# Attention units of a two-block transformer kernel: logits of tiles 0 and 1 in one group, later tiles a period sooner, stick-breaking values by two

## What is computed

```
layer a: gMLP spatial gating + memory attention (4 heads of 64, 256 memory rows) -> w_out -> conv FFN
layer b: forgetting attention (12 heads, causal, decay bias) + memory attention   -> w_out -> conv FFN
layer c: stick-breaking attention (8 heads) + differential attention (4 heads, two maps each,
         ALiBi bias, p1 - lam * p2, RMS norm of the output), both gated by silu   -> w_out
```

## Time and profile before

| | us |
|---|---|
| median of three executions | 1449.86 |
| lowest, highest | 1449.11, 1451.22 |
| the profiled execution | 1451.27 |
| its span from first to last instruction | 1449.5 |
| PE busy | 1438.8 (99%) |
| DVE busy | 961.8 (66%) |
| ACT busy | 669.5 (46%) |

### The profile page before, as it was taken

How to read it: one execution, slowest core, us unless ns; L and a number is a source line. 1 busy time by engine, 2 the same in 40 slices (tenths; PEclk the granted TensorE clock), 3 DMA queues, 4 the chain that set the end, 5 groups by cost and what they waited for, 6 DMA issues and landing times.

```text
span 1449.5 us, 20006 instructions
## 1 busy us (share of the span) xinstructions
PE 1438.8 (99%) x7041; PEld 1151.6 (79%) x7041; DVE 961.8 (66%) x1579; ACT 669.5 (46%) x1100; POOL 41.0 (3%) x82
## 2 busy tenths in 40 slices
PE   8999999999999999999999999999999999999999
PEld 7978888888888887777778888888888877777777
DVE  5656777777766647555556777777677666666774
ACT  7445444444442235445454444444323356665662
POOL 0000000000001110000000000000111000000000
PEclk9999999999999999999999999999999999999999
DMA  6323222332346733212132322323677511112122
GB/s 227 124 96 117 73 90 98 101 97 91 101 138 236 235 112 119 76 59 88 61 100 73 101 90 98 101 90 115 203 241 234 163 56 59 59 58 74 59 82 94
DMA packets 44445, 162.66 MB, mean 112 GB/s; under 512 B 5076, under 2 KB 5844, under 8 KB 44384
## 3 DMA queue, kind: packets, MB, share of 16 engines
q1 hardware_dynamic: 33984, 126.44, 26.5%
q0 software_dynamic: 9104, 33.06, 6.7%
q10 hardware_dynamic: 1296, 2.36, 0.4%
HBM read 159.72 MB, written 2.12 MB: 112 GB/s over the span
## 4 chain that ended last, share of the span: by engine, by line
PE 93%; DVE 4%; DMA 2%; ACT 1%; issue 1%; POOL 0%; ACTq 0%; DVEq 0%; POOLq 0%
PE ps L383 17%; PE ps L384 17%; PE ps L385 17%; PE ps L399 5%; PE ps L401 5%; PE ps L400 5%; PE ps L1872 3%; PE ps L1874 3%; PE ps L1873 3%; PE ps L486 3%; PE ps L563 2%; PE ps L2050 1%; PE ps L551 1%; PE ps L1806 1%; PE ps L1808 1%; DVE wl L309 1%
## 5 line engine op out<-in xcount | busy, mean ns | idle before, releaser
L309 DVE TENSOR_TENSOR wl<-raw,wh 128x1024 fp32r<-128x1024 f32 (+3 forms) x199 | 253.9, 1276 | 119.0 <-ACT wh L303 118.8
L303 ACT CAST wh<-raw 128x1024 fp32r<-128x1024 f32 (+3 forms) x199 | 217.7, 1094 | 228.1 <-PE ps L385 194.8
L383 PE MATMUL ps<-xh,wh 128*128 128x512 f32 x720 | 281.1, 390 | 0.6 <-DVE hb L1416 0.6
L385 PE MATMUL ps<-xh,wl 128*128 128x512 f32 x720 | 280.2, 389 | 0.0
L384 PE MATMUL ps<-xl,wh 128*128 128x512 f32 x720 | 280.1, 389 | 0.0
L383 PEld LDWEIGHTS ps<-xh,wh 128*128 128x128 f32 x720 | 135.1, 188 | 30.0 <-issue 2.0
L384 PEld LDWEIGHTS ps<-xl,wh 128*128 128x128 f32 x720 | 135.1, 188 | 28.3 <-issue 0.5
L385 PEld LDWEIGHTS ps<-xh,wl 128*128 128x128 f32 x720 | 135.1, 188 | 28.2
L399 PE MATMUL ps<-xh,wh 128*128 128x512 f32 x344 | 144.5, 420 | 0.7 <-DVE wl L309 0.7
L383 PE MATMUL ps<-hth,wh 128*128 128x512 f32 x352 | 136.9, 389 | 0.0
L384 PE MATMUL ps<-htl,wh 128*128 128x512 f32 x352 | 136.9, 389 | 0.0
(11 more groups left out here) (310 smaller groups left out, 2337.3 us busy)
## 6 DMA issues: line engine op xcount, KB each, us to landing
raw<-w_a_f SPq DMA_DIRECT2D x44, 512.0 KB, 3.2
raw<-w_b_f SPq DMA_DIRECT2D x44, 512.0 KB, 3.2
row<-w_c_rows POOLq DMA_DIRECT2D x32, 512.0 KB, 4.6
row<-w_ada_rows POOLq DMA_DIRECT2D x24, 512.0 KB, 4.7
raw<-w_a_f SPq DMA_DIRECT2D x16, 704.0 KB, 4.1
raw<-w_b_f SPq DMA_DIRECT2D x16, 704.0 KB, 4.2
raw<-w_b_pair SPq DMA_DIRECT2D x18, 512.0 KB, 3.3
raw<-w_front SPq DMA_DIRECT2D x16, 512.0 KB, 3.3
```

The costliest lines, as they stand in the source:

```text
L303: nc.scalar.copy(wh[:, s, :width], raw[:, s, :width]).then_inc(w_hi, 1)
L309: nc.vector.tensor_tensor(wl[:, s, :width], raw[:, s, :width], wh[:, s, :width].bitcast(F32), ALU.subtract).then_inc(w_lo, 1)
L383: nc.tensor.matmul(dst, a, h(k), start=(k == 0), stop=False)
L385: mm = nc.tensor.matmul(dst, b, h(k), start=False, stop=(k == total - 1))
```

## The change

- `PAIR_AT`, `AHEAD_AT` and `MEM_AT` say in which step the logits of which tile are written. In all units those of tiles 0 and 1 are written at t = 0. `fx` and `df` units write those of tiles 2 and 3 at t = 2 and 4 (before: 4 and 6), memory units both at t = 4 (before: 4 and 6), stick-breaking units at t = 4 and 6 as before. DVE's max (`low`) and ACT's exps (`soft`) follow in the same steps; `norm` (`softplus`), `turned` (`tri`) and `copy` stay where they are.
- `lg_at` puts the second tile of such a pair into the same bank, right of the first, if both fit (128+256 columns, or 256+256). `lg_last` makes the max of the first tile wait until the logits of the second are written too, and in memory units the exps of the first wait for the max of the second.
- The values of stick-breaking units are multiplied by two tiles, at the end of t = 5 and 9; a second buffer `awt` holds the weights of odd tiles.

```
+        PAIR_AT, AHEAD_AT, MEM_AT = {0: (0, 1), 4: (2,), 6: (3,)}, {0: (0, 1), 2: (2,), 4: (3,)}, {0: (0, 1), 4: (2, 3)}
+        def lg_at(i, nk):
+            n0 = nk(i - 1) if i % 2 and nk(i - 1) + nk(i) <= S else 0
+            return slice(n0, n0 + nk(i))
+        def lg_last(i, nk):
+            return i + 1 if i + 1 < TT and lg_at(i + 1, nk).start else i
...
         for t in range(PE_STEPS):
             i, odd = divmod(t, 2)
-            if not odd and i < TT:
-                logits(i)
+            for e in lg_in.get(t, ()):
+                logits(e)
...
-                if not odd:
-                    for s in (2 * i - 2, 2 * i - 1):
-                        if i >= 1:
-                            copy(s)
-                    for s in (2 * i, 2 * i + 1):
-                        if i < TT:
-                            exps(s)
+                if not odd and i >= 1:
+                    copy(2 * i - 2)
+                    copy(2 * i - 1)
+                for e in lg_in.get(t, ()):
+                    exps(2 * e)
+                    exps(2 * e + 1)
...
-                if i < TT:
-                    for s in (2 * i, 2 * i + 1):
-                        norm(s) if odd else maxs(s)
+                for e in lg_in.get(t, ()):
+                    maxs(2 * e)
+                    maxs(2 * e + 1)
+                if odd and i < TT:
+                    norm(2 * i)
+                    norm(2 * i + 1)
...
-                dve.wait_ge(a["logit"], 8 * it + s + 1)
+                dve.wait_ge(a["logit"], 8 * it + 2 * lg_last(s // 2, nk) + s % 2 + 1)
...
-                    if not odd and jj < TT:
-                        soft(2 * jj)
-                        soft(2 * jj + 1)
+                    for e in PAIR_AT.get(t, ()):
+                        soft(2 * e)
+                        soft(2 * e + 1)
...
-                pe_pairs(z, tri, pv, between_last(u), u == 0)
+                pe_pairs(z, tri, pv, between_last(u), u == 0, pv_at={2: (0, 1), 4: (2, 3)})
```

More of the change, by code:

```diff
@@ L481, in norm_factor, with pair_logits @@
             dve.wait_ge(s_r, k + 1)
-        def pair_logits(i, n, q, k, last):
+        PAIR_AT, AHEAD_AT, MEM_AT = {0: (0, 1), 4: (2,), 6: (3,)}, {0: (0, 1), 2: (2,), 4: (3,)}, {0: (0, 1), 4: (2, 3)}
[4 more added lines that the diff above has]
+            return i + 1 if i + 1 < TT and lg_at(i + 1, nk).start else i
+        def pair_logits(i, nk, q, k, last):
             for h in range(2):
-                mm = nc.tensor.matmul(lg[h][:, :n], q(h, i), k(h, n), start=True, stop=last)
+                mm = nc.tensor.matmul(lg[h][:, lg_at(i, nk)], q(h, i), k(h, nk(i)), start=True, stop=last)
             return mm
@@ L490, in turn_bank, with pe_pairs @@
             return lg[1] if a is att["fx"] and it == 5 and s == 7 else tb[s % 2]
-        def pe_pairs(logits, turned, values, between, behind_first=False, pv_at={1: (0,), 2: (1,), 3: (2,), 4: (3,)}):
+        def pe_pairs(logits, turned, values, between, behind_first=False, pv_at={1: (0,), 2: (1,), 3: (2,), 4: (3,)}, lg_in=PAIR_AT):
             for t in range(PE_STEPS):
                 i, odd = divmod(t, 2)
-                if not odd and i < TT:
-                    logits(i)
+                for e in lg_in.get(t, ()):
+                    logits(e)
                 if behind_first and t == 2:
@@ L521, in act_pairs, with dve_pairs @@
                 behind(t)
-        def dve_pairs(maxs, norm, behind, rest=None):
+        def dve_pairs(maxs, norm, behind, rest=None, lg_in=PAIR_AT):
             for t in range(PE_STEPS - 1):
                 i, odd = divmod(t, 2)
-                if i < TT:
-                    for s in (2 * i, 2 * i + 1):
-                        norm(s) if odd else maxs(s)
+                for e in lg_in.get(t, ()):
[4 more added lines that the diff above has]
+                    norm(2 * i + 1)
                 if t == 1 and rest:
@@ L536, in logits @@
             def logits(i):
-                n = nk(i)
-                wait(pe, a["max" if decayed else "exp"], 8 * it + 2 * i)
-                mm = pair_logits(i, n, q, k, not decayed)
+                own = lg_at(i, nk)
+                wait(pe, a["max" if decayed else "exp"], 8 * it + 2 * (i if own.start == 0 else i - 1))
+                mm = pair_logits(i, nk, q, k, not decayed)
                 if not decayed:
@@ L543, in logits @@
                 for h in range(2):
-                    nc.tensor.matmul(lg[h][:, n - P:n], identb, maskq, start=False, stop=True).then_inc(a["logit"], 1)
+                    nc.tensor.matmul(lg[h][:, own.stop - P:own.stop], identb, maskq, start=False, stop=True).then_inc(a["logit"], 1)
             def turned(s):
@@ L566, in values @@
                             mm.then_inc(a["pv"], 1)
-            pe_pairs(logits, turned, values, between, pv_at={2: (0, 1), 4: (2, 3)})
+            pe_pairs(logits, turned, values, between, pv_at={2: (0, 1), 4: (2, 3)}, lg_in=AHEAD_AT if decayed else MEM_AT)
         def two_act(act, a, it, p, pt, nk, behind, rest=None, decayed=False):
@@ L572, in exps @@
                 n = nk(s // 2)
-                act.wait_ge(a["max"], 8 * it + s + 1)
+                act.wait_ge(a["max"], 8 * it + (s if decayed else 2 * lg_last(s // 2, nk) + s % 2) + 1)
                 if decayed:
@@ L586, in copy @@
                 nc.scalar.copy(pt[s // 2 % 2][:, s % 2, :n], turn_bank(a, it, s)[:, :n]).then_inc(a["copy"], 1)
-            act_pairs(exps, copy, behind, rest)
+            act_pairs(exps, copy, behind, rest, AHEAD_AT if decayed else MEM_AT)
         def shifted_max(src, bias, dst, s):
@@ L613, in norm @@
                                         ALU.mult).then_inc(a["norm"], 1)
-            dve_pairs(maxs, norm, behind, rest)
+            dve_pairs(maxs, norm, behind, rest, AHEAD_AT if decayed else MEM_AT)
         def mix_high(act, m, k, src, s_ready, v_ready):
@@ L1153, in weight @@
                     act.wait_ge(Z["tri"], base + s + 1)
-                    wait(act, Z["pv"], base + s - 1)
-                    nc.scalar.activation(aws[:, s % 2, :w], zb[s % 4][:, :w], ACT.Exp).then_inc(Z["a"], 1)
+                    wait(act, Z["pv"], base + s - 3)
+                    nc.scalar.activation((aws, awt)[s // 2 % 2][:, s % 2, :w], zb[s % 4][:, :w], ACT.Exp).then_inc(Z["a"], 1)
                 def high(s):
@@ L2035, in z @@
                     j, w = 3 - jj, (jj + 1) * P
-                    wait(pe, Z["a"], base + 2 * jj - 2)
+                    wait(pe, Z["a"], base + (2 * jj - 2 if jj > 1 else 0))
                     for h in range(2):
@@ L2098, in values @@
                     mm.then_inc(a["pv"], 1)
-                pe_pairs(logits, turned, values, between_last(u))
+                pe_pairs(logits, turned, values, between_last(u), lg_in=AHEAD_AT)
             out_block("c_out", *OUT_EARLY[30])
```

24 lines of the change are left out of this document (12 added, 12 removed).

## The result

The changed kernel takes 1455.20 us (median of five, 1454.68 to 1457.29) where the kernel before, in executions beside it, takes 1449.98: a ratio of 1.0038, with a 95% interval of 1.0026 to 1.0050. By the ratio it is 5.5 us slower (the medians are 5.2 apart); 6.9 were forecast. The profiled execution has a span of 1453.7 us.

The account below looks back on a forecast made before the run. PE, busy 99%, was taken to bound the kernel. Groups -1.8, waits that go -3.3 and waits that come +12.0 gave +6.9 us: median 1456.8 from 1449.86, range 1451.0 to 1460.0 (own range 1453.5 to 1460).

Parts of the forecast that it names:

- Groups of matmuls: On PE, merged values groups save up to 0.25 each, a lost logits entry 0.09; -1.8 us in all.
- The unseen second group: Second logits group behind the first one's mask matmuls, `fx` and stick-breaking units: 0.09 taken, +0.5 us over six `fx` units.
- Waits that go: PE's waits in `fx` (-1.3), for memory units' exps (-1.1) and the first stick-breaking split (-0.8) vanish: together -3.3 us.
- point 3: Forgetting units with 16 blocks: turn of values and third logits wait 0.4 in each of two units, +0.8 us.
- 1. *Memory units.: First transposes wait 1.2 in the first unit of front and layer b (+2.5); layer b's second unit +1.0.
- point 2: Front, t = 6: cast, split and norm come +1.8 later; PE loses 1.1 in each of two units, +2.2, and +0.15.
- 4. *Stick-breaking 2 to 4.: `soft` of tile 1 ahead of `high` of tile 0 on ACT; PE waits 1.1 for a split in each unit, +3.4.
- 5. *Stick-breaking 1.: First cast and low parts come later in the first stick-breaking unit; PE waits +1.4 us, and the old split stall goes.
- 6. *Last differential unit.: Max and exps of tile 3 and the mix precede the norm of tile 2; PE waits +0.55 us.
- A (the covers hold): Rival: DVE and ACT run far enough ahead, none of the 12.0 comes; 1444.8 us, chance 0.06.
- B: Rival, half of it: only memory units' first transposes and stick-breaking splits wait; +1.8, 1451.7 us, chance 0.12.
- C (the lateness spreads): Rival: each stick-breaking and `fx` unit pays about twice, another 5 us; 1461.6 us, chance 0.07.

Follow-up runs that it names:

- experiment 3: Changed kernel with z, `low` and `soft` of stick-breaking units one tile at a time as before, values still by two: 1450.79 us, ratio 1.0005.
- experiment 8: Kernel before plus paired stick-breaking values, paired differential tiles 0 and 1, earlier 16-block forgetting logits, last row product moved, layer b memory tiles 2 and 3 paired: 1446.18 us.
- experiment 6: Kernel before, with only the logits of tiles 0 and 1 written together at t = 0 in the four differential units: 1450.00 us, ratio 1.0000.
- experiment 2: Changed kernel with the memory units of both layers as before, one tile at a time: 1452.34 us, ratio 1.0020.
- experiments 1: Changed kernel with ACT's cast of tile 0 (`high`) ahead of `soft` of tile 1 in stick-breaking units: 1451.32 us, ratio 1.0009.
- experiment 5: Changed kernel with DVE's last weight-row product moved to the end of the first stick-breaking unit, from ahead of its first `low`: 1452.86 us, ratio 1.0019.
- experiment 10: Kernel of experiment 8, with differential units 1 to 3 as in the change, the last with tiles 0 and 1 at t = 0, 2 at t = 2, 3 at t = 6: 1443.83 us.
- Kernels 9: Kernel of experiment 8, with differential units 1 to 3 as in the change and the last as in the kernel before: 1444.99 us, ratio 0.9962.

## Why the prediction came out as it did

The direction, the size (5.5 for 6.9) and the places of the waits were right. Against the prediction's sum of -1.8 - 3.3 + 12.0, the ledger gives -4.1 for groups, -3.5 for waits that went and 12.7 for waits that came (5.0 in all, before rounding). For the waits that came, a unit's measured sum is taken and the other terms are subtracted: the groups' worth as below, and the waits that went as read before. That the sum came within 1.9 of the forecast 6.9 is in part luck: groups that go were priced 2.8 too low, and 1.2 of other terms make up for some of it.

**Groups of matmuls: the step that failed.** The prediction says: "Memory and differential units each lose one entry into a logits group, 0.09". A logits group costs more. PE before (t = 5 and 6 of the second differential unit) and after:

```profile
1347.06 0.60 PE L2096 MATMUL ps<-ptd,vns 128*128 128x128 f32 x4
1347.60 1.13 PE L486 MATMUL ps<-kts,qts 64*128 64x512 f32 x4
1348.66 0.55 PE L2084 MATMUL ps<-kf,pd 128*128 128x128 f32 x3
1348.96 0.48 PE L399 MATMUL ps<-xh,wh 128*128 128x512 f32 x1
```

```profile
1352.39 0.60 PE L2107 MATMUL ps<-ptd,vns 128*128 128x128 f32 x4
1352.84 0.49 PE L2095 MATMUL ps<-kf,pd 128*128 128x128 f32 x3
1353.08 0.49 PE L400 MATMUL ps<-xh,wh 128*128 128x512 f32 x1
```

From the values to the block it is 1.90 with the group and 0.69 without, 1.21 more, of which the columns are 0.86 (two pairs of 512, 0.107 per 128 columns). The rest, 0.35, is what a group costs by being there: by these rows the changes of form and what is lost at its two pairs. I had read just this for the values groups (0.16 besides the entry) and got 0.41 a unit there, which experiment 3 measured at 0.41 to 0.43; for logits I counted the entry alone. And a memory unit loses two groups, not one. PE before and after in the second unit of the front, at t = 2, where neither execution waits:

```profile
106.58 0.39 PE L1808 MATMUL ps<-xh,wl 128*128 128x512 f32 x1
106.90 0.70 PE L486 MATMUL ps<-kma,qma 64*128 64x256 f32 x4
...
107.94 0.48 PE L1806 MATMUL ps<-xh,wh 128*128 128x512 f32 x1
```

```profile
107.68 0.39 PE L1820 MATMUL ps<-xh,wl 128*128 128x512 f32 x1
...
108.27 0.48 PE L1818 MATMUL ps<-xh,wh 128*128 128x512 f32 x1
```

From block to block 1.36 with the group and 0.59 without: 0.77 to 0.78, of which 0.43 are columns, so 0.35. At t = 6 the group stands behind values that use half of the array's columns (128*64), where a change of form is due anyway, and is worth 0.20 (experiment 8). Differential units: -0.34 each (-0.36 in experiment 6) for -0.09. Memory units: 0.55 each, -2.2 in all for -0.4. Together they are 2.8 us below the forecast, more than its distance from the ledger (1.9); 1.08 for 0.54 in forgetting units and 0.7 more of waits that came go the other way, and 0.26 of a wait that went was not foreseen.

**The unseen second group.** Predicted 0.09 between 0 and 0.10. It is there, a little over the bound:

```profile
1230.24 0.28 PE L2053 MATMUL ps<-kb 128*128 128x128 bf16 x2
1230.46 0.70 PE L2050 MATMUL ps<-qts,kts 64*128 64x256 f32 x4
1231.09 0.28 PE L2053 MATMUL ps<-kb 128*128 128x128 bf16 x2
1231.19 0.48 PE L400 MATMUL ps<-xh,wh 128*128 128x512 f32 x1
```

From masks to z it is 0.22, from masks to a block 0.10: 0.12 for the change of form, in line with what the Trainium skill, TensorEngine Tiling (Array Packing), Key Properties, says of draining at a change of mode. A forgetting unit with 24 blocks came to +0.16 to +0.18; the rest, up to 0.06, isn't explained.

**Waits that go.** Those for exps are gone in after (0.32, 0.34 and 0.40 by the starts), and come back in experiment 2, which has the memory units as before. The turn's wait in the 16-block units is gone: the split stands ahead of the last norm as before, but starts at 621.70, 2.4 ahead of the transposes at 624.11 (before, 1.4 ahead of where they were due). -0.31 a unit fits 0.65 for the wait that went and +0.18 for the group with 0.16 of the 0.4 that point 3 had added. That point was too dear by 0.5 in all.

**Waits that come, point by point.**
1. *Memory units.* Predicted 1.2 for the first transposes of the front. The block behind them stands 0.15 later against before than the one ahead, although PE had 0.43 of columns, 0.35 of group and 0.32 of wait less to go through: 1.25. With groups at 0.55 a unit the four units' waits (with point 2) are 2.4, 1.3, 1.3 and 1.0, for 2.3, 1.25, 1.2 and 1.0. Right, by its reasons too: the profile shows four maxes in a row and the exp behind the third. In layer b experiment 8 shows that it takes the pair at t = 0.
2. *Front, t = 6.* Seen in both units (0.76 and 0.77 of idle); with what the transposes lose it is 1.1 by the starts, as predicted.
4. *Stick-breaking 2 to 4.* Place, engine and cause were right (experiments 1 and 3). The price was 1.1; the starts on either side say 1.29, since the profile's idle of 1.13 counts from the modelled end of the last matmul, 0.16 behind the point where the next could have started. Two terms of the point are off a little. The split is late by 1.52 against PE's arrival, for 1.46. And from the end of the split (1238.35) to PE's start it takes 0.14, so of the 0.37 between split and PE before the change 0.23 was cover, not 0.33.
5. *Stick-breaking 1.* Predicted 1.4, measured 1.8 by the ledger (an idle of 1.87). The late cast is the point's reason, and it holds, but the prediction doesn't have the second thing that it takes: the product of the weight row, which stands ahead of `low`, before the change too, with DVE idle for 1.85 until the row had landed. Take away the product and the late cast costs nothing (experiment 5); take away the late cast and, with the row as late or later, 0.2 to 0.6 is left (experiments 6 and 1). The rows that 1.4 was read from had the product in them, ending 5.9 behind the last block ahead of z; in the changed kernel it ends 6.5 behind it, in experiment 2 5.6, and the wait on `tri` follows: 1.87 and 1.02. From the issue of the row's load to the start of its product it is 4.0 us before, 4.6 after, 3.9 in experiment 2; why it varies isn't shown.
6. *Last differential unit.* 0.55 predicted, an idle of 0.56, 0.75 by the ledger with 0.34 for the group. Experiment 10 takes tile 3 alone back to t = 6 and has -0.36 in the unit: it is that tile's max and exps, as said.

**The rivals.** A (the covers hold) is out: the waits came. Kernels 9 and 10 are near its 1444.8 us, but with other parts in them, chosen so that the covers do hold. B's sum (+1.8) is out, since the waits of its points 2, 5 and 6 came. So is C (the lateness spreads): the stick-breaking units lose the same 0.88 each and hand nothing on.

What stays open: why the row's load takes longer in one execution than in another, the last 0.06 of a forgetting unit, the front with its pair at t = 4 alone, and why the pair of experiment 6 costs the last unit 0.33 at its first output block. I read the latter as too little of PE's work ahead of it, since tile 2 at t = 2 removes it: in the last unit that is the one thing in which kernels 8 and 10 differ (+0.27 and -0.36), though units 1 to 3 differ too.

## What to carry to other kernels

When one engine is busy all the time, writing a group of work sooner gains only what the group costs by being there, and that has to be read as a whole, from the work ahead of it to the work behind it. What it costs is decided on the other engines: look in their streams for what the moved work now stands ahead of, as here a cast of 0.5 us that five instructions wait for. Take such a change apart unit by unit with a ledger of starts, keep the parts that gain and undo the others: from one kernel 5.5 us slower came one 6.2 us faster.

## What was not expected of the hardware

- A logits group costs 0.34 to 0.36 us on PE beyond its columns when work on the full array stands ahead of it (blocks, or the 128*128 values of differential units), and 0.20 behind the 128*64 values of the memory units of layer b; the two values groups that go in a stick-breaking unit cost 0.41 to 0.43 together; two logits groups with masks between them cost 0.12 for the change of form (1230.24 to 1231.19 above).
- The profile's idle of PE is 0.16 us less than what is lost between the starts (1.13 against 1.29).
- Rows loaded to one buffer by turns with their product on DVE make a loop that runs at its own pace, 5.0 to 5.5 us a turn: in the kernel before the last products start at 1149.31, 1154.32 and 1159.85, each load issued 0.3 us after the product before, and DVE's idle ahead of them grows from 0.51 to 1.13 to 1.85:

```profile
1154.32 1.23 DVE L1373 SCALAR_TENSOR_TENSOR row<-row,vec 128x1024 f32<-128x1024 f32 x1 [1.13 <-DMA row<-w_c_rows]
...
1159.85 1.23 DVE L1373 SCALAR_TENSOR_TENSOR row<-row,vec 128x1024 f32<-128x1024 f32 x1 [1.85 <-DMA row<-w_c_rows]
```
